# First combine of a two-layer decoder step: next projection's weights requested ahead of the statistics wait, one tile's adds ahead of the last tile's reciprocal

## What is computed

```python
def layer_norm(x, g, b):
    mu = mean(x, axis=-1);  var = mean(square(x - mu), axis=-1)
    return (x - mu) * rsqrt(var + 1e-5) * g + b

def post_norm(x, y, g, b):
    return layer_norm(ALPHA * x + y, g, b)            # ALPHA = 4 ** 0.25

# the end of layer 0
x = post_norm(x, hier_moe(x, ...), ln_g[0, 2], ln_b[0, 2])
# layer 1
mk, mv = split(mem_prompt @ mem_wkv[1])               # does not depend on x
h = x @ fox_w_in                                      # 1024 -> 3072 (q, k, v) and 16 forget gates
q, k, v, fl = split(h, [1024, 2048, 3072])
k_past, v_past = cache_fox_k[page_table], cache_fox_v[page_table]
```

## Time and profile before

| | |
|---|---|
| median of 3 runs | 1666.27 us (1661.2 to 1668.71) |
| profiled execution, its time | 1664.37 us |
| its span, first to last instruction | 1662.4 us |
| mean granted TensorE clock | 0.946 of full speed |
| TensorE busy (matmul) | 1491.2 us, 90% |
| VectorE, ScalarE, GpSimd busy | 518.8, 370.9, 203.6 us: 31%, 22%, 12% |
| DMA | 357.75 MB, mean 215 GB/s |
| chain of waits that ended last | TensorE 79%, VectorE 6%, DMA 5%, ScalarE 4%, issue 3% |

### The profile page before, as it was taken

One profiled execution on the slowest core, in us unless ns is written; L12 is line 12 of the kernel. 1 busy time (PEld: TensorE's weight loads), 2 busy tenths in 40 slices (PEclk: granted clock), 3 DMA queues, 4 the chain that ended last, 5 costly groups with the idle time before them and its releaser, 6 DMA issues.

```text
span 1662.4 us, 21715 instructions
## 1 busy us (share of the span) xinstructions
PE 1491.2 (90%) x8511; PEld 987.3 (59%) x8511; DVE 518.8 (31%) x1075; ACT 370.9 (22%) x854; POOL 203.6 (12%) x241
## 2 busy tenths in 40 slices
PE   7999999999989999995999988989999994989990
PEld 6888888865764333373888753447885583333330
DVE  1421335322471111141524233441523256111114
ACT  0111211132041111141100055650214013111113
POOL 0000000000003323123300000000000000344323
PEclk9999899999999999997999989988999996899995
DMA  8212223354467999836278777842516225899935
GB/s 300 69 55 79 107 93 134 144 181 195 155 254 273 403 393 378 334 141 240 84 258 304 282 263 256 307 160 102 194 70 241 103 76 229 343 388 362 361 127 167
DMA packets 84909, 357.75 MB, mean 215 GB/s; under 512 B 21833, under 2 KB 25449, under 8 KB 58177
## 3 DMA queue, kind: packets, MB, share of 16 engines
q1 hardware_dynamic: 50336, 271.23, 43.2%
q0 software_dynamic: 23584, 48.03, 8.4%
q10 hardware_dynamic: 10889, 37.10, 5.6%
HBM read 403.97 MB, written 33.11 MB: 263 GB/s over the span
## 4 chain that ended last, share of the span: by engine, by line
PE 79%; DVE 6%; DMA 5%; ACT 4%; issue 3%; SPq 1%; POOL 1%; POOLq 0%; ACTq 0%; DVEq 0%
PE PS L617 75%; DMA MKV<-in_moe_w_gu,OVR 2%; PE PS L1176 2%; DMA W<-in_fox_v 1%; DVE EX L1257 1%; DMA O<-in_moe_w_down,OVR 1%; PE PS L698 1%; ACT BIG L2120 1%; PE PS L1035 1%; PE PS L950 1%; PE PS L1198 1%; ACT BIG L2125 1%; DMA W<-y_rows,SLOT 0%; ACT X L1905 0%; DMA W<-in_ab_w_in 0%
## 5 line engine op out<-in xcount | busy, mean ns | idle before, releaser
L617 PE MATMUL PS<-X,W 128*128 128x260 f32 x1264 | 290.9, 387 | 29.1 <-issue 15.9
L617 PEld LDWEIGHTS PS<-X,W 128*128 128x128 f32 x1264 | 240.4, 192 | 69.7 <-issue 28.8
L617 PE MATMUL PS<-O,W 128*128 128x260 f32 x1024 | 230.6, 386 | 2.4 <-DVE O L1634 1.6
L617 PEld LDWEIGHTS PS<-O,W 128*128 128x128 f32 x1024 | 195.0, 191 | 37.6 <-issue 3.4
L1843 ACT ACTIVATE BIG<-PS 128x512 f32<-128x512 f32 (+2 forms) x161 | 75.1, 466 | 318.6 <-PE PS L617 224.5
L617 PE MATMUL PS<-W,BIG 128*64 128x512 f32 x512 | 117.5, 613 | 2.0 <-DVE BIG L1762 2.0
L2337 POOL TENSOR_TENSOR SM<-SM,O 128x5 f32<-128x5 f32 x2 | 0.4, 196 | 836.7 <-DVE SM L1712 836.7
L1767 DVE SCALAR_TENSOR_TENSOR BIG<-BIG,SM,PS 128x256 f32<-128x256 f32 x32 | 15.4, 480 | 246.7 <-ACT BIG L2194 246.7
L617 PE MATMUL PS<-MKV,BIG 128*64 128x512 f32 (+1 forms) x384 | 90.9, 523 | 1.0 <-ACT BIG L1843 1.0
L617 PE MATMUL PS<-W,TMP 128*16 128x512 f32 (+2 forms) x512 | 78.3, 583 | 12.7 <-DMA W<-in_fox_v 12.7
L617 PEld LDWEIGHTS PS<-W,BIG 128*64 128x64 f32 x512 | 36.8, 141 | 71.8 <-issue 71.8
(11 more groups left out here) (326 smaller groups left out, 1857.2 us busy)
## 6 DMA issues: line engine op xcount, KB each, us to landing
W<-in_moe_w_gu SPq DMA_DIRECT2D x64, 1024.0 KB, 10.4
TMP<-in_moe_w_down SPq DMA_DIRECT2D x32, 1024.0 KB, 10.1
W<-in_fox_kt SPq DMA_DIRECT2D x64, 512.0 KB, 5.5
W<-in_fox_v SPq DMA_DIRECT2D x64, 512.0 KB, 5.4
W<-in_mem_kt SPq DMA_DIRECT2D x16, 1024.0 KB, 10.0
W<-in_cache_mem_v SPq DMA_DIRECT2D x16, 1024.0 KB, 8.8
y_rows<-BIG ACTq DMA_DIRECT2D x32, 512.0 KB, 9.0
W<-in_mem_wkv SPq DMA_DIRECT2D x13, 1024.0 KB, 4.9
```

Source lines behind the costliest of these rows:

```text
L617: return nc.tensor.matmul(out, lhsT, rhs, start=start, stop=stop, **kw)
```

## The change

It does four things. SyncE asks for the first four blocks of fox_in ahead of the wait for the statistics. That wait becomes one for the statistics alone, since reciprocals get a semaphore of their own (`z_inv`), and it guards only the page loads. VectorE adds up the next tile between a tile's statistics and its reciprocal. The hooks of kv1 move from positions 8 and 9 to 6 and 8, and ScalarE's copies, roots and scalings are written in an order to match.

```diff
@@ -558,10 +558,12 @@
                     sp.wait_ge(S("dn_acc"), 2 * NR)
                     for n in range(FIRST1 + RING, FOX_IN):
                         load(n)
-                    sp.wait_ge(S("z_mv"), 2 * NT)
+                    for n in range(FOX_IN, FOX_IN + RING):
+                        load(n)
+                    sp.wait_ge(S("z_mv"), NT)
                     key_quad(0)
                     key_quad(1)
-                    for n in range(FOX_IN, FOX_IN + 8):
+                    for n in range(FOX_IN + RING, FOX_IN + 8):
                         load(n)
                     key_quad(2)
                     for i in range(4):
@@ -868,7 +870,7 @@
                 if l == 1:
 
                     proj("kv1", MEMT[1], lambda m, h, pos: pe.wait_ge(S("ld_mem"), 48 + 8 * EARLY) if pos == 0 else None,
-                         {4: z_tail, 8: lambda: z_half(0), 9: lambda: z_half(1)}, NMEM)
+                         {4: z_tail, 6: lambda: z_half(0), 8: lambda: z_half(1)}, NMEM)
                     wait_tr(pe, "z")
 
                     def forget():
@@ -1782,21 +1784,40 @@
                     if i:
                         y_v(i - 1)
 
+                def z_sum(n):
+                    t = ORDER[n]
+                    w = P if t < NCH else NS
+                    z = XT[0:w, t, :]
+                    dve.wait_ge(S(f"yg{t}"), 32)
+                    link(V.scalar_tensor_tensor(z, z, ALPHA, fetched(t, 0), ALU.mult, ALU.add))
+                    link(V.tensor_tensor(z, z, fetched(t, 1), ALU.add))
+
+                def z_invert(n):
+                    t = ORDER[n]
+                    w = P if t < NCH else NS
+                    at = 720 + 4 * t
+                    rs = SM[0:w, at + 2:at + 3]
+                    dve.wait_ge(S("z_sd"), n + 1)
+                    link(V.reciprocal(rs, rs))
+                    V.scalar_tensor_tensor(SM[0:w, at + 3:at + 4], SM[0:w, at:at + 1], -1.0, rs, ALU.mult, ALU.mult).then_inc(S("z_inv"), 1)
+
+                def z_stats(n):
+                    t = ORDER[n]
+                    w = P if t < NCH else NS
+                    z = XT[0:w, t, :]
+                    st, mv = SM[0:w, 628 + 16 * t:640 + 16 * t], SM[0:w, 720 + 4 * t:722 + 4 * t]
+                    V.bn_stats(st[:, 0:6], z[:, 0:512])
+                    link(V.bn_stats(st[:, 6:12], z[:, 512:1024]))
+                    V.bn_aggr(mv, st).then_inc(S("z_mv"), 1)
+
                 if l == 0:
-                    for n, t in enumerate(ORDER):
-                        w = P if t < NCH else NS
-                        z = XT[0:w, t, :]
-                        st, mv, rs = SM[0:w, 628 + 16 * t:640 + 16 * t], SM[0:w, 720 + 4 * t:722 + 4 * t], SM[0:w, 722 + 4 * t:723 + 4 * t]
-                        dve.wait_ge(S(f"yg{t}"), 32)
-                        link(V.scalar_tensor_tensor(z, z, ALPHA, fetched(t, 0), ALU.mult, ALU.add))
-                        link(V.tensor_tensor(z, z, fetched(t, 1), ALU.add))
-                        V.bn_stats(st[:, 0:6], z[:, 0:512])
-                        link(V.bn_stats(st[:, 6:12], z[:, 512:1024]))
-                        V.bn_aggr(mv, st).then_inc(S("z_mv"), 1)
-                        dve.wait_ge(S("z_mv"), 2 * n + 1)
-                        dve.wait_ge(S("z_sd"), NT * l + n + 1)
-                        link(V.reciprocal(rs, rs))
-                        V.scalar_tensor_tensor(SM[0:w, 723 + 4 * t:724 + 4 * t], mv[:, 0:1], -1.0, rs, ALU.mult, ALU.mult).then_inc(S("z_mv"), 1)
+                    z_sum(0)
+                    z_stats(0)
+                    for n in range(1, NT):
+                        z_sum(n)
+                        z_invert(n - 1)
+                        z_stats(n)
+                    z_invert(NT - 1)
 
                 def row(n, k):
                     t = ORDER[n]
@@ -2250,34 +2271,36 @@
                 def z_sd(n):
                     t = ORDER[n]
                     w = P if t < NCH else NS
-                    act.wait_ge(S("z_mv"), 2 * n + 1)
+                    act.wait_ge(S("z_mv"), n + 1)
                     A.activation(SM[0:w, 722 + 4 * t:723 + 4 * t], SM[0:w, 721 + 4 * t:722 + 4 * t], ACT.Sqrt, bias=cst("eps")[0:w, :]).then_inc(S("z_sd"), 1)
                 def z_apply(n):
                     t = ORDER[n]
                     w = P if t < NCH else NS
-                    act.wait_ge(S("z_mv"), 2 * n + 2)
+                    act.wait_ge(S("z_inv"), n + 1)
                     A.activation(XT[0:w, t, :], XT[0:w, t, :], ACT.Identity, scale=SM[0:w, 722 + 4 * t:723 + 4 * t],
                                  bias=SM[0:w, 723 + 4 * t:724 + 4 * t]).then_inc(S("z_rows"), 1)
                 if l == 0:
-                    keep(4)
+                    keep(3)
                     z_sd(0)
+                    keep(1)
                     z_apply(0)
+                    z_sd(1)
                     keep(1)
+                    z_apply(1)
                     tr("z", 0, put_z_tail)
+                    z_sd(2)
                     keep(1)
-                    z_sd(1)
-                    z_apply(1)
-                    keep(2)
-                    z_sd(2)
                     z_apply(2)
+                    z_sd(3)
                     keep(1)
                     z_half(0)
-                    z_sd(3)
                     z_apply(3)
+                    z_sd(4)
                     keep(1)
-                    z_sd(4)
                     z_apply(4)
+                    keep(1)
                     z_half(1)
+                    keep(1)
                     wait_out(act, "kv1")
                     act.wait_ge(S("st_mkv"), 16)
                     store(o["mem_k"][1, :, EARLY:8, :], MK[:, EARLY:8, :], "st_mkv")
@@ -2288,11 +2311,11 @@
                         w = P if t < NCH else NS
                         at = 720 + 4 * t
                         z = XT[0:w, t, :]
-                        act.wait_ge(S("z_mv"), 2 * NT + 2 * n + 1)
+                        act.wait_ge(S("z_mv"), NT + 2 * n + 1)
                         A.activation(fetched(t, 0), z, ACT.Square, bias=SM[0:w, at + 1:at + 2], accum_out=SM[0:w, at:at + 1]).then_inc(S("z_sd"), 1)
                         act.wait_ge(S("z_sd"), NT + 3 * n + 1)
                         A.activation(SM[0:w, at + 2:at + 3], SM[0:w, at:at + 1], ACT.Sqrt, scale=1.0 / D, bias=cst("eps")[0:w, :]).then_inc(S("z_sd"), 1)
-                        act.wait_ge(S("z_mv"), 2 * NT + 2 * n + 2)
+                        act.wait_ge(S("z_mv"), NT + 2 * n + 2)
                         A.activation(z, z, ACT.Identity, scale=SM[0:w, at + 2:at + 3], bias=SM[0:w, at + 3:at + 4]).then_inc(S("z_sd"), 1)
             for n, t in enumerate(ORDER):
                 act.wait_ge(S("z_rows"), NT + n + 1)
```

## The result

| | before | changed |
|---|---|---|
| median of 4 runs each | 1667.15 us (1661.2 to 1668.71) | 1642.2 us (1641.47 to 1648.96) |
| ratio, with its 95% interval | | 0.9866 (0.983 to 0.9902) |
| profiled execution | 1664.37 us | 1642.44 us |
| its span | 1662.4 us | 1640.5 us |
| mean granted TensorE clock | 0.946 | 0.956 |

A forecast was written before the change was run, and what follows sets the result against it. It took TensorE's waits, on late-requested fox_in weights and late statistics, to bound the kernel. 19.95 + 1.35 - 0.9 = 20.4 us off the profiled 1664.37 gives 1644.0; runs' median 1.9 higher, so 1645.9, range 1640 to 1652.

The forecast's parts named there:

- The requests: SyncE's queue: fox_in's blocks 36 to 39 asked for at about 721, 730, 741 and 751, ahead of the page loads.
- The row of VectorE: VectorE's statistics, laid out at 4.3 us a tile, with the last ending at 738.6 against 748.65 before.
- Block 36 beside the gathers, 0.9 us: First fox_in weight block, 1 MB, entering while gathers fill the DMA engines: delays tile 1's second gather, costing 0.9 us.
- the two bounds: Gathers beside block 36: either no delay, or all 1 MB ahead of them, 2.5 us; a cost of 0 to 0.9.
- The clock, 1.35 us: TensorE from 725 to fox_in's first pair: clock 1.00, both pairs alike at 7.2 to 7.3 us; 1.35 us in the sum.
- The cover of the stores, 4 us: Stores of kv1's results before VectorE writes MKV: wanted at 771, landing at 767 even if last, so 4 us spare.
- Rival A: After 751, TensorE comes early to stores or pages that did not move; up to half the gain lost, 1650 to 1657; chance 0.09.
- Rival B: Nothing net: requests don't really move, or a later stretch keeps its own clock; 1658 to 1670, or 1654; chance 0.06.
- Rival C: Short waits from 724.8 on drop TensorE's clock to 0.50 through fox_in's first pair: 29 us slower, 1675; chance 0.02.
- my own sign of being right: TensorE between 707 and the first fox_in product: no wait over 1.5 us.
- the row less block 36: Start of fox_in: 19.95 us earlier by the engines' laid-out order, less 0.9 for the gathers.

The follow-up runs named there:

- weights alone: Kernel before the change, with only the first four fox_in blocks asked for ahead of the old wait for all statistics: 1651.9 us, ratio 0.9878.
- statistics alone: Changed kernel with SyncE's old order, eight page loads ahead of the weight blocks, behind the wait for the five statistics: 1653.04 us, ratio 0.989.
- vector_only: Changed kernel with the old hooks (positions 8 and 9) and ScalarE's old order put back: 1646.31 us; run again unaltered, 1652.36 us.
- four banks again: Second run of the changed kernel with the combine's transposes going through four PSUM banks in place of two: 1642.07 us, ratio 0.9823.

## Why the prediction was right

Point by point, from kv1's start (the prediction laid everything out from 707.3):

- **The requests** at 14.0, 22.7, 33.7 and 43.7 us: measured 14.1, 22.8, 33.7, 43.7. Right, and that is the larger part of the gain (weights alone, 14.6).
- **The row of VectorE**, 4.3 us a tile: 4.2. Last statistics at 31.3: 31.1. Right.
- **TensorE**: tail at 18.2, first half at 26.8, second half at 37.1, fox_in at 43.7: measured 18.5, 26.8, 36.9 and 43.5. The waits were 0.98 and 0.60 where I had 0.7 and 1.0, since tile 0's gather landed 0.3 later than laid out and each tile took 0.1 less.
- **Block 36 beside the gathers, 0.9 us: this is the term that was mis-sized.** It measured 0.2 at most. The block does slow the gathers (9.6 us for the slowest against 6.9), but VectorE went from tile 0 to 1, 2 and 3 without a wait. The step that failed is that the block would hold up tile 1's gathers from its request on, so that tile 1 would land 0.8 late and be waited for. Tile 1's second gather took 7.0 us against 6.7 before and was there 16.9 us after kv1's start, 1.6 ahead of VectorE. The first gather that was held up by more than 0.5 us is tile 2's second, and tiles 2 and 3 had 0.8 and 2.5 us to spare. Of the two bounds I took the upper one, and the lower was nearly right.
```profile
722.09 0.93 POOL L2428 DMA_INDIRECT W<-y_rows,SLOT  x1 [0.30 <-issue]
723.33 0.94 POOL L2428 DMA_INDIRECT W<-y_rows,SLOT  x1 [0.30 <-issue]
```

  The half rate from the request on, which I drew from it, is not what the trace shows.
- **The clock, 1.35 us**: 1.45. Right, and shown to hang on both parts: with weights alone the first pair still took 8.68, with the statistics alone 10.01.
- **The cover of the stores, 4 us**: 7, since they landed 11.0 after the request rather than last of all. Rival A did not occur: TensorE's waits further on are unchanged.
- **Rival B** did not occur: the requests moved. **Rival C**'s mechanism is real, but not its extent: waits of 1.69, 2.83 and 3.85 to 3.92 us lowered the clock to 0.50 in other versions and in the kernel before, for some us, and the positions behind them took 1.5 to 2.7 us longer; it was never 29. Three traces of the changed kernel, with waits of 0.98, 1.69 and 1.71, don't show it. The last two break my own sign of being right (no wait over 1.5 us) and lost nothing by it: that the first trace kept the sign is in part luck.

The sum was 20.4 and the traces give 21.6. fox_in came 20.16 us earlier where the row less block 36 said 19.05: of the 1.1 between them 0.7 is the block and 0.4 the row. The clock gave 0.1 more. The timed difference is larger still, 25, 23.6 and 22.3 us in the three places where both kernels were timed. The late copy may be part of it, since one of two traces of the kernel before has it, at 8 us, and the changed order does not pay for it. How often it falls on the timed runs is not known, and runs of one kernel lie up to 16 us apart, so this part is argued and not shown.

## What to carry to other kernels

When TensorE stands with "issue" as its releaser, read the queue that should have asked for its data: here 15.9 us came from four requests behind a wait that only their neighbours needed, and lifting them past it was worth 14.6. Parts that end the same wait overlap (14.6 and 12.6 alone, 21.6 together), so they have to be priced along one row of events and not added. Put a short operation that a long chain hangs on (a root, a reciprocal) ahead of bulk copies in its engine's queue: it costs nothing when all is on time. With one copy late, TensorE waited 3.85 to 3.92 us before the tail where the root stood behind that copy (three traces) and 1.69 to 1.71 where it stood ahead of it (three traces). The whole change spared the 8 us that the kernel before lost to a late copy; what the root's place gives by itself was not tested.

## What was not expected of the hardware

**A release that comes one position late.** The copy of position 3's result, and SyncE's request for block 36 where it waits for the same count, come at 14.1 us after kv1's start in five of the 13 traces, at 14.8 in two, and at 17.6, with the end of position 4, in six (the second of the kernel before, the second and third of the changed one, statistics alone, both of vector_only). ScalarE and SyncE see it late together, while TensorE's records of these positions run on in all 13 (48 matmul records in 10.52 us) and the copies ahead of it are on time to 0.02 us. The ends of matmuls are modelled in these traces. No run told the cause apart; it stays open.

**The same wait, with and without a lower clock behind it.** After 1.69 us (statistics alone) the granted clock fell to 0.50 for a short while; after 1.69, 1.70 and 1.71 us in the same place in three other traces (changed twice, four banks again) it stayed at 1.00. The 2.32 us before the second half show both outcomes too, in the two traces of vector_only. What decided it was not found.
